# Two-block layer on one core: the twelve later feature products of the input projection spread evenly over the eight recurrence steps

## The reference, cut to what matters

```python
h = rms_norm(x, g_norm1) * (1.0 + scale1) + shift1            # 1024 x 1024
proj = jnp.dot(h, w_in)                                       # 1024 x 2560
x_lru, z_lru, q, k, v = jnp.split(proj, SPLITS, axis=-1)      # five times 512 columns
xc = conv(x_lru, 4 taps) + conv_b
# for each of two directions, in blocks of 64 channels:
r = sigmoid(xc @ w_a + b_a);  i = sigmoid(xc @ w_x + b_x)
a = exp(8 * r * log_sigmoid(lam));  u = sqrt(1 - a**2) * (i * xc)
h_t = a_t * h_(t-1) + u_t                                     # along the sequence
y_lru = (h_fwd + h_bwd) * gelu(z_lru)
```

## Time and profile before

| | |
|---|---|
| median of 3 runs | 2159.48 us (2157.32 to 2161.14) |
| the profiled execution | 2156.82 us, span of its instructions 2155.1 us |
| TensorE matmul busy | 2059.5 us, 96% of the span |
| VectorE busy | 1667.6 us, 77% |
| ScalarE busy | 1083.1 us, 50% |
| mean granted TensorE clock | 0.977 of full |

### The profile page before, as it was taken

The page is one execution under the profiler, slowest core; times in us unless marked ns, Lnnn a source line. Parts: engine busy times, 40 slices in busy tenths (PEclk is TensorE's granted clock), DMA queues, the critical chain, the costliest instruction groups (busy, mean ns, idle before and its releaser), DMA issues. The chain is left out here.

```text
span 2155.1 us, 25072 instructions
## 1 busy us (share of the span) xinstructions
PE 2059.5 (96%) x9904; PEld 1599.1 (74%) x9904; DVE 1667.6 (77%) x1716; ACT 1083.1 (50%) x1240; POOL 233.4 (11%) x170
## 2 busy tenths in 40 slices
PE   6999999999997999999999969999999999999998
PEld 4767855777865888888888757888888874588876
DVE  5575237895567899999999768999999978864776
ACT  4388136893235777777777543112132168523143
POOL 0200010001000111110110140000000014234040
PEclk9999998999998999999999979999999999999999
DMA  7311152004369999999999751111122235433121
GB/s 291 110 40 40 40 189 91 1 1 91 137 272 354 364 386 392 402 392 401 393 400 392 226 189 42 59 59 51 66 79 98 89 141 201 157 127 117 40 79 59
DMA packets 130644, 380.15 MB, mean 176 GB/s; under 512 B 9534, under 2 KB 22110, under 8 KB 130550
## 3 DMA queue, kind: packets, MB, share of 16 engines
q1 hardware_dynamic: 116758, 338.85, 41.4%
q0 software_dynamic: 7568, 23.09, 4.4%
q10 hardware_dynamic: 6224, 16.93, 2.0%
HBM read 335.72 MB, written 43.06 MB: 176 GB/s over the span
## 5 line engine op out<-in xcount | busy, mean ns | idle before, releaser
L2602 DVE SCALAR_TENSOR_TENSOR arena<-arena,vecs 128x1023 f32<-128x1023 f32 (+14 forms) x240 | 304.3, 1268 | 7.1
L2148 DVE TENSOR_TENSOR w_low<-W,w_high 128x2048 fp32r<-128x2048 f32 x96 | 216.9, 2286 | 37.2 <-ACT w_high L2058 37.2
L2148 DVE TENSOR_TENSOR w_low<-arena,w_high 128x2048 fp32r<-128x2048 f32 x96 | 218.4, 2289 | 19.4 <-ACT w_high L2058 19.4
L1887 PE MATMUL Q<-hT_high,w_high 128*128 128x512 f32 (+1 forms) x736 | 230.3, 392 | 1.8 <-DVE hT_low L2131 1.0
L1887 PE MATMUL Q<-hT_low,w_high 128*128 128x512 f32 (+1 forms) x720 | 225.4, 391 | 0.0
L2058 ACT ACTIVATE w_high<-arena 128x2048 fp32r<-128x2048 f32 x96 | 184.2, 1920 | 74.1 <-PE Q L1958 74.1
L2058 ACT ACTIVATE w_high<-W 128x2048 fp32r<-128x2048 f32 x96 | 184.0, 1919 | 73.2 <-PE Q L1958 64.6
L1887 PE MATMUL Q<-hT_high,ring_low 128*128 128x512 f32 x704 | 220.3, 390 | 0.0
L1900 ACT ACTIVATE w_high<-W 128x1024 fp32r<-128x1024 f32 x44 | 46.6, 1058 | 256.0 <-PE Q L1887 243.0
L1958 PE MATMUL Q<-w_high,x_high 128*128 128x512 f32 x512 | 160.2, 394 | 2.4 <-DVE x_low L2151 2.4
L1887 PEld LDWEIGHTS Q<-hT_high,w_high 128*128 128x128 f32 (+1 forms) x736 | 135.5, 184 | 34.5 <-issue 1.6
(11 more groups left out here) (487 smaller groups left out, 4142.5 us busy)
## 6 DMA issues: line engine op xcount, KB each, us to landing
arena<-in_w_dram SPq DMA_DIRECT2D x48, 2048.0 KB, 10.8
W<-in_w_dram SPq DMA_DIRECT2D x48, 2048.0 KB, 11.4
W<-in_w_mod_dram SPq DMA_DIRECT2D x12, 2048.0 KB, 10.3
W<-in_w_in_dram SPq DMA_DIRECT2D x12, 2048.0 KB, 9.1
W<-in_w_out_dram SPq DMA_DIRECT2D x6, 2048.0 KB, 10.5
spill<-arena ACTq DMA_DIRECT2D x24, 512.0 KB, 2.6
W<-in_w_in_dram SPq DMA_DIRECT2D x8, 1024.0 KB, 9.5
arena<-spill SPq DMA_DIRECT2D x3, 2048.0 KB, 12.4
```

The lines of the kernel that those rows point to most:

```text
L1887: ins = nc.tensor.matmul(Q[rows, 2 * pair_of(n) + half, :], w[:, k], x[:, k, HALF * half:HALF * half + HALF], start=k == 0 and w is high a ...
L2148: nc.vector.tensor_tensor(wl[:], chunk_src(r, j), wh[:].bitcast(F32), ALU.subtract).then_inc(low_v, 1)
L2602: ins = nc.vector.scalar_tensor_tensor(conf[:, i, j:], u[:, 0:S - j], w, conf[:, i, j:], ALU.mult, ALU.add)
```

## The change

TensorE's order within the projection is changed, and the orders of ScalarE and VectorE with it. Features 4 to 15 are no longer one per step for eight steps with four behind them: an even step has one feature ahead of its gates, an odd step one ahead and one behind. So the order is 4 g0, 5 g1 6, 7 g2, 8 g3 9, 10 g4, 11 g5 12, 13 g6, 14 g7 15, and then v. The places n are read from a written-out order (`in_order`).

VectorE now makes the rests of a step's features (numbers f + 3) after the recurrence; the first quarter of v comes ahead of recurrence 7, and the other three behind it. ScalarE makes the rounded part of the first quarter of v between the gates of step 7 and its square root.

```diff
-        readers = "v" * 4 + "sss" * STEPS + "s" * 4 + "v" * 8
+        features_of = [[4 + 3 * (j // 2)] if j % 2 == 0 else [5 + 3 * (j // 2), 6 + 3 * (j // 2)] for j in range(STEPS)]
+        in_order = [("feature", f) for f in range(4)]
+        for j in range(STEPS):
+            in_order += [("feature", features_of[j][0]), ("gate", 2 * j), ("gate", 2 * j + 1)]
+            in_order += [("feature", f) for f in features_of[j][1:]]
+        in_place = {what: n for n, what in enumerate(in_order)}
+        readers = "v" * 4 + "s" * (len(in_order) - 4) + "v" * NT
 
         def feature_at(f):
-            return f if f < 4 else 4 + 3 * (f - 4) if f < 4 + STEPS else 4 + 3 * STEPS + f - 4 - STEPS
+            return in_place["feature", f]
+
+        def gate_at(j, g):
+            return in_place["gate", 2 * j + g]
...
                 for j in range(STEPS):
-                    feature(4 + j)
+                    feature(features_of[j][0])
                     if j == 0:
                         pe.wait_ge(gate_in, 8 * 16)
                     gates(j)
-                for f in range(4 + STEPS, FEATURES):
-                    feature(f)
+                    for f in features_of[j][1:]:
+                        feature(f)
...
-                for j in range(STEPS):
+                for j in range(STEPS - 1):
                     recurrence(j)
                     if j + 2 < NLRU:
                         conv(j + 2)
-                    in_rest(7 + j)
-                in_rest(FEATURES - 1)
-                for p in range(KD // 2):
+                    for f in features_of[j]:
+                        if f + 3 < FEATURES:
+                            in_rest(f + 3)
+                in_rest(FEATURES)
+                recurrence(STEPS - 1)
+                for p in range(1, KD // 2):
                     in_rest(FEATURES + p)
...
-                        done = feature_at(FEATURES - 5) + 3 if f == FEATURES else feature_at(f - 4) + 1
+                        done = gate_at(STEPS - 1, 1) + 1 if f == FEATURES else feature_at(f - 4) + 1
...
                 for j in range(STEPS):
-                    evacuate(4 + j)
+                    first = features_of[j][0]
+                    evacuate(first)
                     gates(j)
-                    in_first(7 + j)
+                    if j == STEPS - 1:
+                        in_first(FEATURES)
+                    elif first + 3 < FEATURES:
+                        in_first(first + 3)
                     act.wait_ge(ratio_ready, j + 1)
                     nc.scalar.activation(t_r, t_r, ACT.Sqrt).then_inc(root_ready, 1)
-                evacuate(4 + STEPS)
-                in_first(FEATURES - 1)
-                for f in range(5 + STEPS, FEATURES):
-                    evacuate(f)
-                    if f == 5 + STEPS:
-                        in_first(FEATURES)
-                    in_first(FEATURES + f - 4 - STEPS)
+                    if j == STEPS - 1:
+                        in_first(FEATURES + 1)
+                        in_first(FEATURES + 2)
+                    for f in features_of[j][1:]:
+                        evacuate(f)
+                        if f + 3 < FEATURES:
+                            in_first(f + 3)
+                in_first(FEATURES + 3)
```

More of the change, by code:

```diff
@@ L487, in gates @@
                     for g in range(2):
-                        n = 5 + 3 * j + g
+                        n = gate_at(j, g)
                         pair_free(pe, n)
@@ L752, in gates @@
                             .then_inc(proj_s, 1)
-                    act.wait_ge(proj_s, 3 * j + 3)
+                    act.wait_ge(proj_s, readers[:gate_at(j, 1) + 1].count("s"))
                     c0 = NLRU * d + m
```

## The result

The changed kernel takes 2165.88 us (median of 11 runs), the kernel before beside it 2157.72 us (median of 11): ratio 1.0039, 95% interval 1.0027 to 1.0050. One of the eleven runs took 5314.81 us; the ratio leaves it out. The change costs 8.4 us by the ratio (0.0039 x 2157.72) and 8.2 by the two medians. The forecast was 8.3 us slower, with TensorE standing 5.9 us in the first v tile and 2.4 us lost to a lower clock behind it.

What follows compares the result with a forecast made beforehand. The prediction took TensorE to bound the kernel from gates 0 to the last v tile. Order 0, stall 5.9 and lower clock 2.4 summed to 8.3 us on 2159.48, so 2167.8 us, range 2161.5 to 2172.0.

Steps and rivals of the forecast that it cites:

- TensorE alone sets the pace, and its order costs nothing: From gates 0 to the last v tile, TensorE is the limit; the new order moves its sum of matmuls by 0.
- The steps have no new wait: Within the recurrence steps, every feature's inputs come in time, the tightest with 3.7 us of slack; cost 0.
- Recurrence 7 ends 20.61 us behind gates 7: At the end of the steps, recurrence 7, started by gates 7 at 232.69, ends at 253.30, its ratio delayed by 2.09 us.
- The stall, 5.9 us: In the first v tile TensorE waits 5.9 us for quarter 1, made behind recurrence 7 on VectorE; bounds 4.8 to 6.9.
- The clock, 2.4 us: Behind the stall TensorE's granted clock is at half for a while, costing 2.4 us, the middle of 1.9 to 2.85.
- The sum, 8.3 us and 2167.8: Whole kernel: 0 + 5.9 + 2.4 = 8.3 us added to the median before, 2159.48, gives 2167.8 us; chance 0.62.
- Drift behind the stage, 1.7 us for each of two places: In the next stage, two low-clock stretches may fall differently against the work, 1.7 us to either side for each.
- The 0.27 us per round: In the projection, each round of gates and feature costs TensorE 0.27 us extra; the count stays, so the change is 0.
- the clock that stays up: Rival: behind the stall the clock stays up or its cost is given back later; 5.9 us alone, 2165.4; chance 0.21.
- more than one stall: Rival: in_rest(8) also comes late, a second stand of some 2 us with 1.9 us of low clock; 2171.7, chance 0.07.
- no stall: Rival: recurrence 7 ends in time, quarter 1 is ready by 248.7 and TensorE never stands; 2159.5, chance 0.07.
- faster: Rival: the 0.27 us were gate matmuls waiting for ScalarE, removed by the new order; 2.2 us less, 2157.3, chance 0.03.

Runs made afterwards that it cites:

- e1: Changed kernel with the four v quarters prepared earlier, three ahead of recurrence 7 on VectorE; gates 0 to last v copy 194.08 us, ratio 0.9992 against the kernel before.
- e4: Changed kernel without the last two VectorE operations of recurrence 7, so TensorE stands for less time (3.30 us); ratio 1.0034 against the kernel before.
- e5: Changed kernel with two more additions on VectorE behind recurrence 7, so TensorE stands longer (8.34 us); ratio 1.0062 against the kernel before.
- e3: Changed kernel with 24 matmuls into an unread bank while TensorE would stand for quarter 1; ratio 1.0032 against the kernel before.
- e6: Kernel before, old order kept, with five additions on VectorE ahead of the last v quarter to make TensorE stand (5.54 us); ratio 1.0036 against the kernel before.
- e2: Changed kernel with the rests of v quarters 1 and 2 made inside recurrence 7, giving stands of 0.98 and 4.08 us; ratio 1.0038 against the kernel before.
- the order by pairs: Against the kernel before, gates of both directions stand side by side, four rounds of gates and features instead of eight; ratios 1.0020 and 0.9996 in two timings.

## Why the prediction was right

- *TensorE alone sets the pace, and its order costs nothing.* Right: e1's stage is equal to 0.01 us.
- *The steps have no new wait.* Right; feature 8 and the others came in time, and ScalarE's wait for the end of the recurrence (5.7 us) is gone from the list of waits and bought nothing. The reading of that list was short by two lines of the same view: ScalarE also waited 2.1 us for even recurrences (VectorE's L639), and two more starts of a weight load were 0.6 us late (ScalarE's L741). Neither held a matmul back.
- *Recurrence 7 ends 20.61 us behind gates 7.* 251.30 - 230.62 = 20.68. From gates 7 the ratio started at 12.19, 2.17 us later than in step 1, and the second product at 14.61, 1.19 later; the rest was taken up by the table load, as reckoned (2.09 and 1.13).
- *The stall, 5.9 us.* Measured 5.83, and e4 and e5 show that its chain is the one named.
- *The clock, 2.4 us.* 2.43 by the rows after, 2.32 by e3. That a stand of this length brings the clock down was right. That the cost came out at the middle of the range is in part luck: it was taken from the lengths of three other stands, but in e4 to e6 it goes from 1.8 to 2.9 us with the low time that meets work, which the prediction had no way to know. The Trainium skill, "TensorE: Matmul & The Clock Gate", section "Terms", takes the penalty as the throttled time times one minus the clock's share. An estimate by it from the low time at work, 5.0 us, is 2.5, and the trace agrees within 0.1; from the whole low stretch of 6.8 us it would be 3.4, too much, since TensorE stood for 1.8 of them.
- *The sum, 8.3 us and 2167.8.* 8.4 by the ratio, 8.46 by the stage. The median came out 1.9 us lower, at 2165.88; that of before had itself moved from 2159.48 to 2157.72 with more runs. The 2.8 us that the range adds to either side are less than the drift (twice 1.7) and the spread (2) named for it add up to.
- *Drift behind the stage, 1.7 us for each of two places.* Too small for single executions: the next stage alone varied by 6.7 us. The medians show no drift beyond their noise, but a single execution could have left the range by it.
- *The 0.27 us per round.* Too small as the price of a round: four rounds less gave 1.65, or 0.41 each. Two gate pairs side by side took 7.01 us and not twice 3.58, so the gate pair's price held 0.15 of it. It played no part in the forecast, where their number stayed.

The rivals: the clock that stays up is ruled out by e3 and the rows after; more than one stall by the list of waits; no stall and faster by the result. That the clock's cost is given back behind the stage, 5.9 us in all, isn't ruled out by the timing of the changed kernel alone, whose interval begins at 5.8 us. Against it speak the ratios of e2, e4, e5 and e6: at 1.0034 to 1.0062 none is clearly smaller than its stage alone makes it (1.0029 to 1.0047).

## What to carry to other kernels

Where one engine is busy without a gap, spreading its work more evenly over another engine's chain has no gap to fill (e1 gained nothing here), and it can use up the cover that the unspread work gave to the end of that chain. Ask what the last link has behind it: here four features had hidden recurrence 7 and the quarters that queue behind it on VectorE, and one feature didn't. Price a stand of TensorE with what its clock takes afterwards, 1.8 to 2.9 us on top of each single stand from 3.3 to 8.3 us here: about half of the low time in which it works. Compare variants by the length of the stage between two marks in the trace. That of the order by pairs was 192.43 us in both its profiles, on two chips, while its ratio moved by 0.24%.

## What the runs showed that I had not expected

- A stand of 3.30 us cost more behind it (2.93 us) than one of 8.34 us (1.82 us), because more of its low stretch met work. The clock fell 2.1 to 5.2 us after TensorE's stop, latest not at the longest stand but at that of 4.08 us.
- At a stand of 4.08 us (e2) the clock fell about 1.1 us after TensorE had started again: 0.50 us for the matmul at 258.17, 0.63 from 259.58.
- A stage of the same instructions took 43.7 to 50.4 us with a mean granted clock of 0.96 to 0.83. The Trainium skill, "TensorE: Matmul & The Clock Gate", section "What's actually happening", says that the clock's monitor runs free of the kernel's start; no run here shows the monitor itself, but the spread agrees with it. And an interval of twelve runs (1.0004 to 1.0035) left out 1 for a kernel that then measured 0.9996 on the other chip: with such a spread one interval just clear of 1 is no proof.
